# A three-block transformer kernel on one core: first unit in pieces, splits inside waiting parts, another norm for the convolution, last units by token halves

## What is computed

```python
# latent attention (layers 0 and 1): queries and keys come from normalised latents
q = rms_norm(c_q, q_norm_g) @ w_uq
kv = rms_norm(c_kv, kv_norm_g) @ w_ukv
# block 2, attention: p = exp(s - m); o = (p @ v) / (sum(p) + exp(sink - m))
# block 2, convolution: 31 taps over tokens, then a norm over 512 channels
y = conv(u * sigmoid(gate)) + conv_b
mu = mean(y, channels); var = mean((y - mu) ** 2, channels)
out_b = silu((y - mu) * rsqrt(var + EPS) * ln_g + ln_b)
# feed-forward
x = x + (silu(h2 @ w_gate) * (h2 @ w_up)) @ w_down
```

## Time and profile before

| | us |
|---|---|
| median of 3 runs (lowest to highest) | 2020.97 (2020.75 to 2021.65) |
| the profiled execution | 2020.23 |
| its span, first to last instruction | 2018.6 |
| TensorE busy | 1990.5 |
| VectorE busy | 1126.6 |
| ScalarE busy | 951.1 |
| POOL busy | 76.1 |
| DMA, mean over the span | 179 GB/s |

### The profile page before, as it was taken

How to read it: one execution, slowest core, us unless ns; L and a number is a source line. 1 busy time by engine, 2 the same in 40 slices (tenths; PEclk the granted TensorE clock), 3 DMA queues, 4 the chain that set the end, 5 groups by cost and what they waited for, 6 DMA issues and landing times.

```text
span 2018.6 us, 27772 instructions
## 1 busy us (share of the span) xinstructions
PE 1990.5 (99%) x10292; PEld 1685.6 (84%) x10292; DVE 1126.6 (56%) x1317; ACT 951.1 (47%) x1271; POOL 76.1 (4%) x124
## 2 busy tenths in 40 slices
PE   9999999999999999999999899999999999999998
PEld 7898988888889998888877777788888888888886
DVE  5484555556566454655747796544545444444443
ACT  5365444444464454444665655544444444443432
POOL 3000000001100000000200100000000000000000
PEclk9999999999999999999999999999999999999999
DMA  8574455665755444666555335566666666656563
GB/s 277 188 228 126 148 163 165 191 194 161 246 178 179 148 151 138 206 188 188 154 156 167 125 126 167 178 189 190 192 188 187 188 188 191 192 172 220 202 207 106
DMA packets 187752, 360.78 MB, mean 179 GB/s; under 512 B 13169, under 2 KB 19872, under 8 KB 187392
## 3 DMA queue, kind: packets, MB, share of 16 engines
q1 hardware_dynamic: 182832, 345.62, 55.0%
q0 software_dynamic: 4816, 13.76, 2.5%
HBM read 357.23 MB, written 2.10 MB: 178 GB/s over the span
## 4 chain that ended last, share of the span: by engine, by line
PE 91%; DVE 4%; ACT 2%; DVEq 1%; issue 1%; ACTq 0%; POOL 0%; DMA 0%; POOLq 0%
PE psum L615 24%; PE psum L617 24%; PE psum L616 24%; PE psum L623 3%; PE psum L626 3%; PE psum L625 3%; DVE wl L573 1%; DVE conv_y L831 1%; PE psum L977 1%; PE psum L703 1%; PE psum L678 1%; PE psum L689 1%; PE psum L1181 1%; PE psum L855 1%; PE psum L1405 0%
## 5 line engine op out<-in xcount | busy, mean ns | idle before, releaser
L573 DVE TENSOR_TENSOR wl<-raw,wh 128x1024 fp32r<-128x1024 f32 (+1 forms) x656 | 777.0, 1196 | 687.4 <-ACT wh L565 680.3
L565 ACT ACTIVATE wh<-raw 128x1024 fp32r<-128x1024 f32 (+1 forms) x656 | 672.5, 1036 | 829.3 <-PE psum L617 691.9
L615 PE MATMUL psum<-wh,xh 128*128 128x512 f32 (+2 forms) x1600 | 621.5, 388 | 5.2 <-DVE wl L573 4.3
L617 PE MATMUL psum<-wh,xl 128*128 128x512 f32 (+2 forms) x1600 | 615.2, 384 | 0.0
L616 PE MATMUL psum<-wl,xh 128*128 128x512 f32 (+2 forms) x1600 | 614.7, 384 | 0.0
L615 PEld LDWEIGHTS psum<-wh,xh 128*128 128x128 f32 x1600 | 300.6, 188 | 67.7 <-DVE wl L573 5.5
L617 PEld LDWEIGHTS psum<-wh,xl 128*128 128x128 f32 x1600 | 300.5, 188 | 59.3
L616 PEld LDWEIGHTS psum<-wl,xh 128*128 128x128 f32 x1600 | 300.8, 188 | 57.3
L615 PE MATMUL psum<-wh,mh 128*128 128x512 f32 x376 | 148.1, 394 | 3.2 <-DVE wl L573 3.1
L617 PE MATMUL psum<-wh,ml 128*128 128x512 f32 x376 | 146.4, 389 | 0.0
L616 PE MATMUL psum<-wl,mh 128*128 128x512 f32 x376 | 146.4, 389 | 0.0
(11 more groups left out here) (368 smaller groups left out, 1532.8 us busy)
## 6 DMA issues: line engine op xcount, KB each, us to landing
raw<-in_w_in_dram SPq DMA_DIRECT2D x264, 512.0 KB, 4.4
raw<-in_w_out_dram SPq DMA_DIRECT2D x96, 512.0 KB, 3.7
raw<-in_w_gate_dram SPq DMA_DIRECT2D x88, 512.0 KB, 3.6
raw<-in_w_up_dram SPq DMA_DIRECT2D x88, 512.0 KB, 3.6
raw<-in_w_down_dram SPq DMA_DIRECT2D x80, 512.0 KB, 3.6
cmp_raw<-in_cmp_w_dram SPq DMA_DIRECT2D x16, 512.0 KB, 4.6
raw<-in_w_small_dram SPq DMA_DIRECT2D x16, 336.0 KB, 3.1
bias<-in_b_in_dram POOLq DMA_DIRECT2D x18, 256.0 KB, 3.9
```

The source lines that it names most:

```text
L565: act.activation(wh[:, n % SPLIT_SLOTS, 0:k, 0:unit.n], buffer[:, 0:k, 0:unit.n], ACT.Copy).then_inc(hi_done, 1)
L573: dve.tensor_tensor(out=wl[:, n % SPLIT_SLOTS, 0:k, 0:unit.n], in0=buffer[:, 0:k, 0:unit.n], in1=wh[:, n % SPLIT_SLOTS, 0:k, 0:unit.n].bit ...
L615: pe.matmul(o, ah_[:, kt, tok], hi_w, start=first, stop=False)
L617: ins = pe.matmul(o, al_[:, kt, tok], hi_w, start=False, stop=last)
```

## The change

- **First unit in pieces.** The first unit's two tiles are loaded and split one by one, and x's first block in two halves. TensorE runs 8 idle products, turns the first two tiles of x, 6 idle products, multiplies the first half of unit 0, turns the other two tiles, multiplies the second half; block 1 of x is turned in the middle of unit 1.
- **Splits inside waiting parts.** In the layers one split of slot 2 is held back and made within part 1, while POOL works. In block 2 each softmax part makes the next slot's first split, on ScalarE between exponentials and scaling, on VectorE behind the reciprocal.
- **The taps** are dealt out anew: fewer in front of part 11 and in it, more behind parts 17 and 19 and slot 22.
- **The convolution's norm by tokens.** The mean uses 1/512 as the summing matrix. The squares are summed with `conv_sq` as the stationary operand and one moving column, so that the sums lie by token in [128 x 2]. POOL takes the root; VectorE puts the factors on a diagonal; a new stage 24 spreads them over partitions.
- **Block 2's end.** The turned tiles of stages 28 to 30 alternate between two halves of `st`; VectorE's low parts of x go behind part 28, behind the last unit's split and behind part 31; the feed-forward network's first split goes ahead of part 30, the others follow one by one.
- **The last four units** are multiplied for the first 128 tokens, then for the others; each half is added and stored by itself, by SP.

```diff
-TAPS_AT_SLOT = {11: (1,), 12: (1, 1, 1, 1), 14: (1, 1, 1, 1), 16: (1, 1), 19: (1,)}
-TAPS_AT_MID = {10: 1, 12: 1, 14: 3, 15: 2, 16: 1, 17: 2, 18: 1, 19: 2}
-TAPS_IN_MID = {11: 2, 13: 1, 17: 2, 19: 1}
+TAPS_AT_SLOT = {11: (1,), 12: (1, 1, 1), 14: (1, 1, 1, 1), 16: (1,), 22: (0, 0, 2)}
+TAPS_AT_MID = {10: 1, 12: 1, 14: 3, 15: 1, 16: 1, 17: 3, 18: 1, 19: 4}
+TAPS_IN_MID = {11: 1, 13: 1, 17: 2, 19: 1}
...
@@ -902,9 +894,16 @@
                 act_operand(place, name, 0)
                 act_operand(place, name, 1)
             else:
-                for n in range(2):
-                    act_operand(place, name, n)
-                    split_high(place, n, units[n])
+                act = nc.scalar
+                act.wait_ge(raw_first, 16)
+                act.activation(wh[:, 0, 0, :], raw[:, 0, 0, :], ACT.Copy).then_inc(first_high, 1)
+                act.wait_ge(s(name + "_turned"), 1)
+                x_high(0, all_banks[:, x_column(0):x_column(0) + T])
+                x_high(1, all_banks[:, x_column(1):x_column(1) + T]).then_inc(s(name + "_high"), 1)
+                act.wait_ge(raw_loaded[0], 16)
+                act.activation(wh[:, 0, 1, :], raw[:, 0, 1, :], ACT.Copy).then_inc(hi_done, 1)
+                split_high(place, 1, units[1])
+                act_operand(place, name, 1)
             for n in range(2, PARTS):
...
@@ -922,9 +921,20 @@
             def split(n):
                 split_low(place, n, units[n])
             if not updates:
-                for n in range(2):
-                    operand(n)
-                    split(n)
+                dve = nc.vector
+                def first_low_part(kk):
+                    return dve.tensor_tensor(out=wl[:, 0, kk, :], in0=raw[:, 0, kk, :], in1=wh[:, 0, kk, :].bitcast(F32),
+                                             op=ALU.subtract)
+                dve.wait_ge(first_high, 1)
+                first_low_part(0).then_inc(first_low, 1)
+                dve.wait_ge(s(name + "_high"), 1)
+                x_low(0, all_banks[:, x_column(0):x_column(0) + T]).then_inc(s("first_operand"), 1)
+                x_low(1, all_banks[:, x_column(1):x_column(1) + T]).then_inc(s(name + "_operand"), 1)
+                dve.wait_ge(hi_done, 1)
+                first_low_part(1).then_inc(lo_done, 1)
+                split(1)
+                operand(1)
...
-                    pe_idle_products(*((8, True) if updates else (12, False)))
+                    pe_idle_products(8, True)
                 nc.tensor.wait_ge(s(name + "_operand"), PARTS * (place.once - 1) + n + 1)
+        def pe_first_units(place, units):
+            pe = nc.tensor
+            pe_idle_products(8, False)
+            block_0 = pe_turn_block("pre", 0, 0)
+            next(block_0)
+            pe_idle_products(6, False)
+            def first(kk):
+                if kk == 0:
+                    pe.wait_ge(first_low, 1)
+                    pe.wait_ge(s("first_operand"), 1)
+                else:
+                    next(block_0)
+                    pe.wait_ge(s("pre_operand"), 1)
+                    pe.wait_ge(lo_done, RAW_SLOTS + 1)
+            def second(kk):
+                if kk == 0:
+                    pe.wait_ge(s("pre_operand"), 2)
+                    pe.wait_ge(lo_done, RAW_SLOTS + 2)
+                else:
+                    for _ in pe_turn_block("pre", 0, 1):
+                        pass
+            multiply(place, 0, units[0], pieces=first)
...
+                sp.dma_start(x[:, :, c0:c1], d["x"][0].rearrange("(b p) n -> p b n", p=P)[:, :, c0:c1])\
+                    .then_inc(loaded, 16)
+            def load_first():
+                src = weight_src(LAYER_SLOTS[0][0], 0, *LAYER_SLOTS[0][0].pieces[0])
...
                 place = in_layer(l)
                 for n in load_order():
-                    if l == 0 and n in (0, 2, 3, 4):
-                        load_x(max(n - 1, 0))
...
                             "(t p) n -> p t n", p=P)[:, unit.kts[0]:unit.kts[-1] + 1,
                                                      bass.ds(i * (2 * GN) + g * GN, GN)])
-            sp.wait_ge(out_stored, 16 * 4)
+            sp.wait_ge(s("last_rows_ready"), 1)
+            sp.dma_start(out[0:P, 3 * GN:], x[:, 0, 3 * GN:]).then_inc(last_stored, 16)
...
+            pool.wait_ge(s("conv_ms2"), 1)
+            stand_alone(pool, "pool")
+            pool.tensor_tensor(out=conv_ms[:, 1, :], in0=conv_ms[:, 0, :], in1=minus_half.to_broadcast([P, TB]),
+                               op=ALU.pow).then_inc(s("conv_rstd2"), 1)
...
-                    pool.dma_start(out[:, bass.ds(i * (2 * GN) + g * GN, GN)].rearrange("(b p) n -> p b n", p=P),
-                                   x[:, :, bass.ds(i * (2 * GN) + g * GN, GN)]).then_inc(out_stored, 16)
+            for i, g in ((0, 0), (0, 1), (1, 0)):
+                pool.wait_ge(dve_mid_done, down_place(i).slots + g + 2)
+                cols_ = slice((2 * i + g) * GN, (2 * i + g + 1) * GN)
...
                 for j in range(4):
-                    ins = pe.matmul(st[:, 1536:1536 + T], one.to_broadcast([P, P]), src[:, j, :], start=j == 0,
+                    ins = pe.matmul(st[:, 1536:1536 + T], inv_512.to_broadcast([P, P]), conv_y[:, j, :], start=j == 0,
                                     stop=j == 3)
                 return ins
+            def token_sums():
+                for tb in range(TB):
+                    for j in range(4):
+                        ins = pe.matmul(st[:, 1536 + tb:1537 + tb], conv_sq[:, j, tb * P:(tb + 1) * P], one,
+                                        start=tb == 0 and j == 0, stop=j == 3, skip_group_check=True)
+                return ins
+            def factor_rows():
+                for tb in range(TB):
+                    ins = pe.matmul(st[:, 1536 + tb * P:1536 + (tb + 1) * P], one.to_broadcast([P, P]),
+                                    conv_stat[:, tb, :], start=tb == 0, stop=True, skip_group_check=True)
...
-                22: lambda: sum_channels(conv_y), 23: lambda: sum_channels(conv_sq),
+                22: channel_means, 23: token_sums, 24: factor_rows,
...
                         turn_last_x()
+                    if first and n == 4:
...
+                units = list(enumerate(down_units(1)))[DOWN_UNITS - LAST_ROWS:]
+                for tb in range(TB):
+                    tok = slice(tb * P, (tb + 1) * P)
+                    for j, unit in units:
+                        n, (kt,) = DOWN_UNITS + j, unit.kts
+                        o, hi_w, lo_w = acc[1][:, tb, :], wh[:, n % SPLIT_SLOTS, 0, :], wl[:, n % SPLIT_SLOTS, 0, :]
+                        if tb == 0:
+                            pe.wait_ge(lo_done, RAW_SLOTS + pl.units + n + 1)
+                        pe.matmul(o, ah[:, kt, tok], hi_w, start=False, stop=False)
+                        pe.matmul(o, ah[:, kt, tok], lo_w, start=False, stop=False)
+                        ins = pe.matmul(o, al[:, kt, tok], hi_w, start=False, stop=unit.last)
+                        if tb:
+                            ins.then_inc(unit_used, 1)
+                    if tb == 0:
+                        ins.then_inc(s("last_first_rows"), 1)
...
+                place = splits.place
                 act_mid(place, 0, len(slots[0]), mids.get(0, nothing))
-                n = len(slots[0]) + len(slots[1])
+                n = splits.n
                 for h in range(2, len(slots)):
                     done = n
-                    for unit in slots[h]:
-                        split_high(place, n, unit)
-                        after_unit.get(n, nothing)()
-                        n += 1
+                    n += len(slots[h])
+                    while splits.n < n - held.get(h - 1, 0):
+                        splits.next()
                     act_mid(place, h - 1, done, mids.get(h - 1, nothing))
...
                                            accum_out=sq_sums[:, 2 * tb + i:2 * tb + i + 1])
                     act.drain().then_inc(s("mla_sums"), 1)
+                    splits.next()
...
+                }, {1: 1}, ahead_of_last)
...
                 if sink:
                     act.activation(sink_e, sink_e, ACT.Exp).then_inc(s(name + "_sink"), 1)
+                splits.next()
...
-            def first_ffn_splits():
-                for n in range(SLOT_UNITS):
-                    split_high(ffn_place(0), n, units[n])
-            after_unit[unit_of_2(25, 1)] = conv_rstd
-            after_unit[unit_of_2(CONV_SLOT, 0)] = lambda: (conv_silu(), act.drain(), conv_high())
...
+            def ffn_split(n):
+                split_high(ffn_place(0), n, units[n])
+            after_unit[unit_of_2(31, 0)] = lambda: ffn_split(0)
+            after_unit[unit_of_2(26, 1)] = lambda: (conv_silu(), act.drain(), conv_high())
...
-            }, first_ffn_splits)
+            }, ahead=lambda: ffn_split(1))
+            ffn_split(2)
+            ffn_split(3)
...
             def conv_centre():
```

(38 more changed lines are left out.)

169 lines of the change are left out of this document (99 added, 70 removed).

## The result

The change took 19.5 us off: median 2001.65 us (2001.27 to 2001.98) against 2021.18 for the kernel before in the same lot, ratio 0.9904 with a 95% interval of 0.9892 to 0.9916. The profiled execution took 2001.57 us, its span 1999.8.

A forecast was written before the change was run, and what follows sets the result against it. TensorE, busy for 99% of the span, was taken as the bound. Terms of 0.7, 1.36, 4.7, 1.1, 2.2 and 1.7 sum to 11.8: from 2020.2 to 2008.4, plus 0.8 to the median, 2009.2 us; range 2006.3 to 2013.4.

The forecast's parts named there:

- The end: Last addition and store: shorter half addition, SP issuing sooner, store landing 1.3 to 1.9 us earlier; 1.7 us taken.
- the moved taps: Taps moved behind parts 17, 19 and slot 22: covered by products, cost nothing; without cover up to 3.4 us.
- Parts 7 and 13: Block 2 softmax: split inside wins 1.13 us of TensorE's wait, costs 0.45; 0.65 and 0.7 won.
- Part 11: Block 2 softmax: about 2.4 us sooner covers the 2.01 wait, plus 1.12 for the split: 3.1 us won.
- Start and latents: First units: third unit at 16.9 instead of 17.65, 0.7 us; layer 0's stage 2 wait gone, 1.36 us.
- the passage: Passage into the FFN: first FFN split done at 1277.7 instead of 1279.9; 2.2 us won, ends 1.2 and 3.1.
- The low end of 0.3 for the norm: Convolution's norm, forecast 1.1 us won: only 0.3 if sums take 0.19 a record, the full weight load.
- Gains shrink: Rival, chance 0.22: part 11's end stays and the passage gives only 1.2; gain 8.8, time 2012.2 us.
- only the covered part acts: Rival, chance 0.03: stops reappear one unit later, ends and latents remain; 3.1 and 0.7 won, 2017.2 us.
- split blocks the softmax: Rival, chance 0.02: late loads hold ScalarE's split and everything behind it in six parts, 19.8 us; time 2029.
- All goes: Rival, chance 0.05: 14.5 us won, time 2006.5 us.
- The clock falls: Rival, chance 0.06: at the start, fewer warming products leave 18 products 0.23 us dearer each, 4.1 us; time 2013.3.

The follow-up runs named there:

- before_new_taps: The kernel before with the new tables of taps alone, splits still behind the softmax parts: 2019.16 us, ratio 0.9996 (0.9987 to 1.0005).
- after_no_split: The kernel after without the splits inside the six softmax parts, the new taps kept: 2008.21 us.
- after_pool_store: The kernel after with both half stores of the last column group issued by POOL instead of SP: 2005.88 us.
- before_sp_store: The kernel before with the last column group stored whole by SP instead of POOL: 2015.58 us, ratio 0.9975.
- after_whole_store: The kernel after with the last four units and last addition for all 256 tokens at once and one 512 KB store by SP: 2002.57 us.
- after_old_taps: The kernel after with the convolution's taps dealt out by the three tables of before: 2007.04 us.

## Why the prediction was wrong

**The end, 1.7 for 5.8.** The failed step is "2009.94 + 0.23 + (2.5 to 3.1) is 2012.7 to 2013.3, against 2014.6". It compares landings. Behind the landing in the kernel before lay 4.0 us to the end of the span (2014.6 to 2018.6), and the sum kept them without saying so. They were POOL's closing drain, and they go when POOL has no store late in the program. Both numbers were at hand: the span, and the earlier trace rows with 3.1 from issue to landing. The range took the landing's bounds and gave this stretch none: it shrank from 4.0 to 0.5. The landing's own term was too small as well. Counted from the addition's start the last store landed 5.3 behind it before and 3.05 after, 2.25 less, outside the 1.3 to 1.9: the store of 256 KB took 2.3 by SP, less than the 2.5 of the load that was to bound it from below, and SP issued 0.05 behind the addition. The estimate of 2.6 for such a store fits POOL's (2.6) and not SP's.

**Slot 17, 0 for 2.1.** The failed step is the list of stops itself. The earlier trace rows have 8 waits for low parts, 7.4 us in all; those that the prediction placed in the text sum to about 5.6. The 1.8 left over was this stop (1.82). With it came the second failed step, "the moved taps ... I cost them at nothing": taken from one place and put in another, they moved two stops. The cost was 0.9 ahead of stage 21, not the 3.4 of the bound and not at slot 22 but behind part 19, where the sentence on taps had looked for no cover at all.

**Parts 7 and 13, 0.65 and 0.7 for 0.89 and 1.60.** The split inside a part was priced at 0.45 (a split of 1.06 less 0.62 of idle time). It starts 0.1 behind the sinks' exponential, while VectorE still makes the sum, and delays the scaling by 0.23 at part 7 and 0.14 at part 13. And "its taps are the same" was true of part 13 and not of the queue in front of it: VectorE entered it with 2.2 us of backlog instead of 2.9. This gain needs new taps and splits together: with the old taps the kernel after loses 0.6 at part 13, and with the new taps but no splits inside the parts (before_new_taps and after_no_split) the wait ahead of its transposes stays at 1.63.

**Part 11, right for half a reason.** 3.1 was forecast as 2.0 for the taps and 1.1 for the split. Taps alone gave 2.85 (before_new_taps), and taking the split away cost 0.29; taking the taps away cost 2.0. Both remove the same lateness, so neither has a price of its own.

**The step from the profiled execution to the median, 0.8 for 0.1.** The sum ended at 2008.4 and added 0.8, as the median had lain above the profiled execution before. In the kernel after it lies 0.1 above (2001.65 against 2001.57): another 0.7 of the miss. Why, no run shows.

**What held.** Start and latents 2.06 for 2.22, though inside the start the steps were off: the first product came at 8.84 and not 9.3, as the gains landed earlier than 7.1 (ScalarE goes on at 4.35). The start's share of the 2.22 is not firm either: the third unit begins at 17.65, 18.53 and 18.71 in the three traces with the old start. Stage 2 then waits 1.20, 0.49 and 0.60, which evens most of it out. Part 5, the passage (2.2 for 2.17) and the sums over channels: 16 records with one moving column took 1.84 beside 1.89 for 8 with 256, and 1.70 by distance. Stage 24 cost 0.36, less than the 0.5. The low end of 0.3 for the norm does not come out of its own sum: 16 records of 0.19 are 3.0 against 1.7, which leaves a loss of 0.2.

**The rivals.** "Gains shrink", "only the covered part acts" and "split blocks the softmax" did not happen; no wait for a load stands in the six parts. "All goes" came nearest, at 2006.5, and was too small too, as it lacked the two missed terms. "The clock falls" did not happen at the start of the kernel after, yet its mechanism is real: the run without warming products has it there, and two runs have it behind stops of 1.81 and 1.83 us in block 2. No waits of this length are left in the kernel after; that some executions of before lost time in this way is possible and was not shown, since neither its trace nor the two traces of kernels made from it have such a fall.

Not tried on their own: the convolution's norm, the order of the last slots and the pieces of the first unit. For these the comparison of the two traces stands alone.

## What to carry to other kernels

Add up the stops you have placed and set them against the table of waits, and the last landing against the end of the span: what is left over in either is a term you have not seen. Let the queue that needs the longest to close (here POOL's, 6.8 us after a store) issue nothing late. Work dealt out over an engine's gaps and work moved ahead in its queue are one change, not two; move them together, and then look again at each part's entry; the last 1.8 us here were found so.

## What the hardware showed

- POOL's closing drain took 6.75 to 6.77 us when the program's last store was its own, of 512 or 256 KB (before, before_new_taps, after_pool_store), and ended 3.8 to 4.1 us behind the landing. Where SP stored last, the span ended 0.5 behind the landing.
- The last store of the program took, from issue to landing, 2.3 us by SP and 2.6 by POOL with 256 KB, and 2.7 by SP (before_sp_store, after_whole_store) and 3.1 by POOL with 512 KB.
- After stops of 1.81 and 1.83 us TensorE's granted clock was 0.62 in the next 4.5 us, and the products were 0.43 apart instead of 0.23: 1.6 to 1.7 us on top of the stop. After six other stops of 1.80 to 1.84 us (two each in before and before_sp_store, one in before_new_taps, one ahead of part 11 in after_old_taps) it stayed at 1.00. The Trainium skill, "TensorE: Matmul & The Clock Gate" (Part 1), has the clock go back to half after idleness; two of these eight stops were followed by that and six were not, so a stop of 1.8 us is a risk and not a rule. What tells the two from the six, no run here shows.
- The same start gave a first product between 8.00 and 8.99 us in nine traces, by how early the clock rose.
